# Row dots ahead of the first root, four modulation buffers and earlier attention constants in a two-layer hybrid trunk

## What is computed

```
sh1, sc1, g1, sh2, sc2, g2 = split(silu(c) @ ada_w + ada_b, 6)
h = rmsnorm(x) * (1 + sc1) + sh1
y = mlstm_conv_mixer(h)     # layer 0: 4 mLSTM heads beside a gated convolution
y = stick_breaking_mixer(h) # layer 1: 16 heads of strictly causal attention
x = x + (1 + g1) * y
h = rmsnorm(x) * (1 + sc2) + sh2
x = x + (1 + g2) * peer_ffn(h)
...
# stick breaking, per head and 128-query block
log_1mb = where(strict, log_sigmoid(-z), 0)
between = cumsum(log_1mb, reverse=True) - log_1mb
att = where(strict, exp(log_sigmoid(z) + between), 0)
```

## Times and profile before

| | us |
|---|---|
| median of three runs | 3181.23 |
| the three runs | 3168.26, 3181.23, 3183.55 |
| the profiled execution, own time | 3175.37 |
| its span, first to last instruction | 3173.6 |
| PE busy, of the span | 3082.9 (97%) |
| DVE busy | 2692.0 (85%) |
| ACT busy | 1497.6 (47%) |
| POOL busy | 1549.9 (49%) |

### The profile page before, as it was taken

One profiled execution on the slowest core, in us unless ns is written; L12 is line 12 of the kernel. 1 busy time (PEld: TensorE's weight loads), 2 busy tenths in 40 slices (PEclk: granted clock), 3 DMA queues, 4 the chain that ended last, 5 costly groups with the idle time before them and its releaser, 6 DMA issues.

```text
span 3173.6 us, 44402 instructions
## 1 busy us (share of the span) xinstructions
PE 3082.9 (97%) x15444; PEld 2690.9 (85%) x15444; DVE 2692.0 (85%) x4862; ACT 1497.6 (47%) x2678; POOL 1549.9 (49%) x896
## 2 busy tenths in 40 slices
PE   6999999999999999999999999999999999999999
PEld 4777899999999888888777567999999998888887
DVE  5678897999998988888775658998999998888887
ACT  3233334666665333333444753346666663333332
POOL 3324345899988422322232014357988875222221
PEclk9999999999999999999899999999999999999999
DMA  5543235999999999999434023357999999999996
GB/s 222 201 145 113 80 118 184 310 344 338 367 325 361 390 378 365 359 370 367 150 100 132 1 73 107 98 174 262 365 329 320 375 328 373 349 352 349 345 347 239
DMA packets 312488, 833.52 MB, mean 263 GB/s; under 512 B 26624, under 2 KB 147472, under 8 KB 312160
## 3 DMA queue, kind: packets, MB, share of 16 engines
q1 hardware_dynamic: 181552, 422.62, 37.9%
q0 software_dynamic: 74000, 268.81, 23.6%
q10 hardware_dynamic: 56736, 139.49, 11.7%
HBM read 735.91 MB, written 94.90 MB: 262 GB/s over the span
## 4 chain that ended last, share of the span: by engine, by line
PE 62%; POOL 21%; issue 8%; DVE 5%; DMA 2%; ACT 1%; SPq 0%; POOLq 0%; DVEq 0%; ACTq 0%
PE banks L1002 22%; POOL w_lo L491 13%; PE gbank L1002 11%; POOL u_rows L508 9%; PE banks L962 3%; PE banks L963 3%; PE banks L964 3%; PE banks L983 3%; PE banks L982 3%; PE banks L984 3%; DVE u_rows L1771 2%; DMA u_rows<-u_dram,row_of 2%; DVE hot L1748 1%; PE gbank L1197 1%; PE gbank L1302 1%
## 5 line engine op out<-in xcount | busy, mean ns | idle before, releaser
L491 POOL TENSOR_TENSOR w_lo<-raw,w_hi 128x1024 fp32r<-128x1024 f32 x355 | 874.6, 2465 | 763.2 <-ACT w_hi L554 759.6
L554 ACT ACTIVATE w_hi<-raw 128x1024 fp32r<-128x1024 f32 x613 | 649.7, 1060 | 863.0 <-PE banks L1002 569.6
L982 PE MATMUL banks<-h_hi,w_hi 128*128 128x384 f32 x2048 | 691.3, 338 | 16.6 <-ACT gel L743 13.9
L983 PE MATMUL banks<-h_lo,w_hi 128*128 128x384 f32 x2048 | 686.8, 335 | 0.0
L984 PE MATMUL banks<-h_hi,w_lo 128*128 128x384 f32 x2048 | 686.7, 335 | 0.0
L516 POOL DMA_INDIRECT v_rows<-v_dram,row_of x256 | 286.2, 1118 | 728.9 <-DVE fetched L1786 712.8
L1771 DVE CUSTOM_DVE_ANT_0 u_rows<-u_rows,h_rows 128x1024 f32<-128x1024 f32 x256 | 462.9, 1820 | 25.9 <-DMA u_rows<-u_dram,row_of 25.7
L508 POOL DMA_INDIRECT u_rows<-u_dram,row_of x256 | 380.9, 1488 | 102.5 <-DVE z L1771 61.1
L982 PEld LDWEIGHTS banks<-h_hi,w_hi 128*128 128x128 f32 x2048 | 386.1, 189 | 25.1 <-issue 16.1
L983 PEld LDWEIGHTS banks<-h_lo,w_hi 128*128 128x128 f32 x2048 | 385.9, 188 | 0.0
L984 PEld LDWEIGHTS banks<-h_hi,w_lo 128*128 128x128 f32 x2048 | 385.8, 188 | 0.0
(11 more groups left out here) (330 smaller groups left out, 4895.1 us busy)
## 6 DMA issues: line engine op xcount, KB each, us to landing
raw<-stream_dram SPq DMA_DIRECT2D x613, 512.0 KB, 5.7
gel_dram<-gel ACTq DMA_DIRECT2D x248, 192.0 KB, 4.9
gin<-gel_dram SPq DMA_DIRECT2D x62, 768.0 KB, 10.4
g_dram<-stage ACTq DMA_DIRECT2D x56, 768.0 KB, 10.3
gates<-g_dram SPq DMA_DIRECT2D x64, 672.0 KB, 7.1
ada_w<-ada_dram ACTq DMA_DIRECT2D x50, 512.0 KB, 4.8
ada_out<-ada_dram ACTq DMA_DIRECT2D x18, 512.0 KB, 4.7
ada_first<-ada_dram SPq DMA_DIRECT2D x8, 1024.0 KB, 19.0
```

Source lines behind the costliest of these rows:

```text
L491: pool.tensor_tensor(w_lo[:, s, :], raw[:, s, :], w_hi[:, s, :].bitcast(F32), ALU.subtract).then_inc(split_lo, 1)
L554: act.activation(w_hi[:, s, :], raw[:, s, :], ACT.Copy).then_inc(split_hi, 1)
L982: pe.matmul(out, wh, h_hi[:, k, 0:DENSE_T], start=(k == 0), stop=False)
L983: pe.matmul(out, wh, h_lo[:, k, 0:DENSE_T], start=False, stop=False)
```

## The change

It has three parts. `DOTS_AHEAD` becomes 4, so `first_dots(2)` and `(3)` stand before the root. A second pair of buffers, `ada_more`, is placed over the tail of `hw`; load `n` now waits for dot `n - 4`, and the loads start one tile sooner, so they go out two tiles ahead of their dots. ACT waits once, at tile 5, until all eight low parts of the first norm are made, since `hw` is read till then. Attention's two constants are made right after the norm of layer 1.

```diff
-DOTS_AHEAD = 2
+DOTS_AHEAD = 4
...
+    assert place[0] <= arena + 80 * KB
+    place[0] = arena + 80 * KB
+    ada_more = sb("ada_more", [P, 2, D])
...
-        def ada_load(n, off=0):
-
-            wait(act, S("ada_used"), n - 1 + off)
-            src = ada[ds(2 * DC + n + off, 1), :, :].rearrange("a p n -> p (a n)")
-            act.dma_start(ada_w[:, n % 2, :], src).then_inc(S(f"ada{n % 2}"), 16)
+        def ada_load(n):
+
+            b = n % 4
+            wait(act, S("ada_used"), n - 3)
+            act.dma_start((ada_w, ada_more)[b // 2][:, b % 2, :], ada[2 * DC + n]).then_inc(S(f"ada{b}"), 16)
...
-            if ADA_FROM <= m < ADA_FROM + 15:
-                ada_load(2 * (m - ADA_FROM) + 2)
-                ada_load(2 * (m - ADA_FROM) + 3)
+            if m == ADA_FROM - 1:
+                act.wait_ge(S("norm_lo"), normed("n0", "lo") + DC)
+            if ADA_FROM - 1 <= m < ADA_FROM + 14:
+                ada_load(2 * (m - ADA_FROM) + 4)
+                ada_load(2 * (m - ADA_FROM) + 5)
...
         norm("n1")
+
+        act.activation(negtri_r[:], negtri[:], ACT.Copy)
+        act.activation(negones_r[:], ones[:], ACT.Copy, scale=-1.0).then_inc(S("neg"), 1)
...
         act.preload_act_table_set("natural_log_exp_and_others")
-        act.activation(negtri_r[:], negtri[:], ACT.Copy)
-        act.activation(negones_r[:], ones[:], ACT.Copy, scale=-1.0).then_inc(S("neg"), 1)
...
         def first_ada(n):
 
-            ada_dot(n, mod[:, 0, 2 * DC + n:2 * DC + n + 1])
+            b = n % 4
+            dve.wait_ge(S(f"ada{b}"), 16 * (n // 4 + 1))
+            ada_dot((ada_w, ada_more)[b // 2][:, b % 2, :], mod[:, 0, 2 * DC + n:2 * DC + n + 1])
```

More of the change, by code:

```diff
@@ L570, in _ @@
         act.dma_start(small_in[1][0], small_in[1][1]).then_inc(S("c_landed"), 16)
-        def ada_load(n, off=0):
-            wait(act, S("ada_used"), n - 1 + off)
-            src = ada[ds(2 * DC + n + off, 1), :, :].rearrange("a p n -> p (a n)")
-            act.dma_start(ada_w[:, n % 2, :], src).then_inc(S(f"ada{n % 2}"), 16)
+        def ada_load(n):
+            b = n % 4
+            wait(act, S("ada_used"), n - 3)
+            act.dma_start((ada_w, ada_more)[b // 2][:, b % 2, :], ada[2 * DC + n]).then_inc(S(f"ada{b}"), 16)
         def v_ada_load(i):
-            n = 4 * DC + i
             act.wait_ge(S("ada_used"), 4 * DC + V_COL + max(i - 1, 0))
-            act.dma_start(ada_w[:, n % 2, :], ada[6 * DC + V_COL + i]).then_inc(S(f"ada{n % 2}"), 16)
+            act.dma_start(ada_w[:, i % 2, :], ada[6 * DC + V_COL + i]).then_inc(S(f"ada{i % 2}"), 16)
         def spare_load(tile, col, first, i):
@@ L1356, in link, with ada_dot @@
             dve.wait_ge(S("dve_link"), links[0])
[L1358 to L1363, removed]
+        def ada_dot(row, dst):
+            dve.tensor_tensor_reduce(row, row, cvec[:], 1.0, 0.0, ALU.mult, ALU.add, dst).then_inc(S("ada_used"), 1)
         def v_mod_dot(i):
-            n = 4 * DC + i
-            ada_dot(n, mod[:, 1, V_COL + i:V_COL + i + 1])
+            dve.wait_ge(S(f"ada{i % 2}"), 16 * (DC + i // 2 + 1))
+            ada_dot(ada_w[:, i % 2, :], mod[:, 1, V_COL + i:V_COL + i + 1])
         def spare_dot(tile, col, r):
```

## The result

| | before | after |
|---|---|---|
| median, us | 3178.44 (9 runs) | 3158.74 (9 runs) |
| fastest and slowest, us | 3168.18, 3183.55 | 3151.45, 3167.68 |
| profiled execution, own time | 3175.37 | 3166.52 |
| its span | 3173.6 | 3164.7 |
| ratio of the times | | 0.9944, 95% interval 0.9929 to 0.996 |

The changed kernel is faster by 17.8 us as the ratio has it (12.7 to 22.6), that is by 0.56%. Both kernels issue the same 15,444 matmuls in the same order, so the two traces can be laid on one another matmul by matmul. The table has the start of a matmul in the changed kernel less its start before.

A forecast was written before the change was run, and what follows sets the result against it. It took the kernel to be bound by a chain of waits between engines with no date of its own. Terms of 4.0, 9.8 and 2.8 summed to 16.6 us; from a middle of 3178.3 it predicted 3161 us, range 3147 to 3175.

The forecast's parts named there:

- First part: First norm: two more blocks of dots move into DVE's idle time before the root, two row blocks lose theirs, -4.0 us.
- The cover of 1.6 us: Before the root: DVE would be ready at 32.6 us, the squares at 34.24, leaving 1.6 us to spare.
- Second part: Mixer of layer 0: loads two tiles ahead end PE's 4.78 us idle time and the clock's fall behind it, -9.8 us.
- Head 0 then looks like head 1: Mixer of layer 0: without idle time and clock fall, head 0 shortens from 37.90 to 32.84 us, 5.06 us won.
- Third part: Attention's start: early constants let the logits start 1.8 us sooner, and the clock falls later, -2.8 us in all.
- the stretch of 0.50 a little later or shorter: Sign expected in the changed kernel's profile at attention's start, where the stretch was 1725.2 to 1738.8 us before.
- that one more us beside the 1.8: Attention's start: one us more, since the clock should fall later without the 2.5 us of idle time before the logits.
- Rival 1: Attention's start: the clock holds, worth -5.1 us there, -18.9 in all, 3159 us; chance 0.15.
- Rival 2: Mixer, tile 12: ACT doesn't catch up, PE still waits some 2 us and the clock falls; -11.2, 3167 us; chance 0.17.
- Rival 3: Start: the third or fourth block's weights land later and the root waits; 4 us late gives -14, 3164 us; chance 0.08.
- Rival 4: Mixer: dots meet POOL's splitting of weight tiles and DVE becomes what a tile waits for; +16, 3194 us; chance 0.04.
- If the time that is won at 205 us is given back before the span's end: Named sign of a wrong prediction: the gain standing behind the mixer's heads is lost later, which no wait read would do.

The follow-up runs named there:

- e7_swap: The changed kernel with attention's log weights put ahead of the weighted values in each head; ratio to the kernel before 1.0091 (1.0064 to 1.0117).
- e11_after: The changed kernel itself run and profiled once more, nothing altered; ratio to the kernel before 0.9948 (0.9928 to 0.9968).
- run 78: Not a label but a count: the unchanged kernel before was run 78 times beside the experiments; its runs spread from 3163 to 3191 us.

## Why the prediction was right

The forecast was 3161 us, within 3147 to 3175; the median is 3158.7. The gain was put at 16.6 us and measured at 17.8 (12.7 to 22.6) and, once more, 16.5 (10.2 to 22.9). That these agree within about 1 us is closer than such intervals can show, so it is partly luck; that each term is right is read from the traces.

- **First part, -4.0.** Measured -4.04, and -3.99 alone. The cover of 1.6 us behind 32.6 was 1.52 behind 32.68. PE fell behind at blocks 4 and 5 as foreseen, for it has no wait there any more, but still waited 0.17 us for the last `h_hi`, so that cost nothing. All eight blocks move the root to 44.21 (44.0 forecast) and give the part's gain back, which confirms the cover as the term that decides; for a fifth block one execution can't tell.
- **Second part, -9.8.** Measured -9.5 (-4.5 to head 0, -5.07 in it). The step "Head 0 then looks like head 1" came out exactly, 32.83 us for 32.84. Of head 0's length, only 3.2 of the 5.07 us are the clock; 1.87 are two waits of PE in the head, which the term took in without naming them. The missing 0.3 us come from a new wait that I did not name either: at tile 10 PE waits 0.62 to 0.69 us for POOL's low part in ten of the eleven profiles with four buffers, and in none of the three without (first row below). In the eleventh, e7_swap, whose kernel is the same up to attention, the wait is missing, and head 0 starts 0.98 us sooner than in after (second row). POOL's split meets DVE's dots about there. One reading was too simple: ACT's waits for dots did not go away, 22.3 us of them were left between 66 and 135 us for 31.7 before. Eight dots in that stretch take 2.3 to 3.4 us each, all of them beside POOL's splits, the others 1.2, so ACT still waits for DVE. PE needed only 4.8 us, and had them.

```profile
102.70 0.50 PE L967 MATMUL banks<-h_hi,w_hi 128*128 128x512 f32 x1 [0.68 <-POOL w_lo L494]
```
```profile
125.08 0.49 PE L1108 MATMUL gbank<-ident,kT 128*128 128x128 f32 x3
```

- **Third part, -2.8.** Measured 1.73 at head 0 (1.8 forecast) and 3.0 at head 2. Expected was "the stretch of 0.50 a little later or shorter": in after it came later, 2.6 us behind the first logits instead of 1.3. Its length went with the execution: 10.2 us in three of the five profiles with early constants, 13.7 and 23.9 in the two of after; 13.7 in four and 17.1 in one of the five with late ones. In the whole time the term isn't resolved, and that one more us beside the 1.8 was the right size rests on head 2 alone.
- **Rival 1, the clock holds at attention's start:** false. It fell in every profile, and the first stretch of 0.50 stayed even with dense matmuls among the logits. The Trainium skill (TensorE: Matmul & The Clock Gate, Part 1: The HAM clock gate) has activity of the engine release the throttled state. If the profile's busy time is that activity, the trace doesn't agree: the row 1710.00:1733.70 has PE busy in all of its 23.70 us at 0.50. The busy time that the profile shows doesn't tell when the clock holds; the two dense kernels hint that the kind of matmul counts in the steady state, and don't prove it.
- **Rival 2, ACT doesn't catch up:** false, PE's wait at head 0 is 0, and tile 12 was copied out 4.6 us before it was needed.
- **Rival 3, weights land late:** false, no wait for `ada_first`, and the fourth block starts at 29.85. Its price was also mis-sized: with the rows' 2.5 us of room, a landing 4 us late moves DVE by 1.5 us, which the cover of 1.6 us takes in, so by its own rows it would have cost next to nothing, not 2.5 us.
- **Rival 4, dots beside POOL's splits make DVE the bound:** its mechanism is there (dots of 2.3 to 3.4 us, ACT waiting for them), its condition isn't: DVE is busy 26.25 us of head 0's 32.83.
- **The middle from which I predicted** (3178.3, of four executions) proved good: nine runs have 3178.4. Less 16.6 us it gives 3161.7, which I put down as 3161. Had I taken the three runs' median, the forecast would have been 3164.6.
- **"If the time that is won at 205 us is given back before the span's end"** was named as a sign of error. In the profiled execution 4.7 of 13.6 us were given back, and the forecast was right nonetheless: the sign is no good for a single profile, since stretches at half clock come and go by several us from one execution to the next.

## What to carry to other kernels

Where an engine idles ahead of its next dense work, price together the idle time, the clock behind it and the waits that follow: here the end of a wait of 4.8 us won 9.5. Work that is moved into idle time is free as far as the releaser's date allows, so compute that date first. A change of under a per cent is read best by laying two traces on one another, instruction by instruction; its whole time only says whether something else went wrong.

## What the runs showed of the hardware

In attention TensorE's granted clock fell to 0.50 (1.2 GHz) while the profile has the engine busy all the time, for instance behind 3.40 us, most of them logits, at 1.00. With one matmul of 128x128 by 256 columns in each head, which costs 0.17 us, 1 head of 13 had such a fall, with three none, where eleven other profiles have 2 to 7. Whether the kind of matmul or the changed length of a head did it is open. At attention's start the clock stayed at 0.50 through 5.20 us of 128x128 log weights, and six matmuls of 128x128 by 128 columns ahead of each group did not prevent the fall. Why the first stretch stays, 10 to 24 us long in all profiles, was not settled.

Where PE waits for `gel`, waits of 2.09 and 2.29 us were followed by 3.4 us at 0.50, and one of 2.61 us (at 739.2) was not (e11_after).

A dot of 128x1024 on DVE takes 1.2 us by itself; in the mixer of layer 0 eight of them, all beside POOL's split of a weight tile, took 2.3 to 3.4 us.

Before's kernel, run 78 times beside these experiments, has a mean granted clock and a time that go together: 3.7 us less for each 0.001 of clock, correlation -0.70. Its runs spread from 3163 to 3191 us, and what the fit leaves is 4.5 us of standard deviation. So about half of the variance of the time goes with the clock. The two traces of the changed kernel show where such differences arise: in where PE's short waits fall, and whether the clock falls behind them.
